# Building the gate matrix of a sparse expert layer with accumulating indirect DMAs instead of one-hot products on TensorE

## The chip, the cores and the metric

The program runs on one core of a Trainium2 chip. A core has TensorE (PE in the rows) for matrix products, VectorE (DVE), ScalarE (ACT), GpSimd (POOL) and SyncE (SP), which share an on-chip memory of 128 partitions (SBUF), PSUM banks for products, and 16 DMA engines. DMAs are issued here by SP (plain loads) and by POOL (gathers by index, and others). The metric is the device time of the whole program in microseconds (us), lower being better.

## The reference, cut to what matters

One decoder layer on 256 tokens of width 2048: a retention group and a sparse-attention group share an input projection, their outputs go through an output projection, and a PEER layer follows. Only the PEER layer is touched. Every token picks, for each of 8 heads, 16 of 128 x 128 experts; expert (i, j) has a row of `u` and a row of `v`.

```python
def peer_ffn(x, wq, subkeys, u, v):
    q = (xt @ wq).reshape(n, PEER_HEADS, 2, PEER_DQ // 2)
    s = jnp.einsum('nhpd,pkd->nhpk', q, subkeys)
    sv, si = lax.top_k(s, PEER_TOPK)
    cand = sv[:, :, 0, :, None] + sv[:, :, 1, None, :]
    cidx = si[:, :, 0, :, None] * PEER_NKEYS + si[:, :, 1, None, :]
    cs, ci = lax.top_k(cand.reshape(n, PEER_HEADS, PEER_TOPK * PEER_TOPK), PEER_TOPK)
    eidx = jnp.take_along_axis(cidx.reshape(...), ci, axis=-1)
    gate = jax.nn.softmax(cs.astype(jnp.float32), axis=-1)
    # per chunk of tokens:
        hid = jax.nn.gelu(jnp.einsum('cd,chkd->chk', xc, u[ec]))
        return jnp.einsum('chk,chkd->cd', gc * hid, v[ec])
```

## The kernel before, in words

**Two ways for the tokens.** 192 tokens (`TD`) are computed densely: all 16384 experts are multiplied with them, and the result is weighted with a gate matrix that is zero where an expert was not picked. The other 64 (`TS`) are computed sparsely: the rows of `u` and `v` that they picked are gathered from DRAM, 128 rows (1 MB) at a time, and VectorE multiplies them.

**The stages of the PEER part.** The 128 values of j are taken in two halves of 64. A half has 64 `u` blocks and then 64 `v` blocks. A `u` block loads 1 MB into one of four `raw` buffers and multiplies it with the tokens (`u_block`, L918, in the first half); ScalarE writes its GELU into `hidden` (L1285). A `v` block loads 1 MB, ScalarE and VectorE split it into a rounded part and a rest (L1318, L1932), and TensorE multiplies both with the gated `hidden` (L1009 to L1021). The gated `hidden` reaches TensorE through `wm`: ScalarE's `round_gated` and VectorE's L1986 and L1987 write it.

**The routing.** During the first 64 `u` blocks VectorE picks the experts. `route_tokens(1, 0)` takes tokens 128 to 255 first, with no gathers between; `route_tokens(0, 14)` takes tokens 0 to 127 and works off 14 gathers (items) at points spread through it (`share`). A token's choice is i (`choice[:, 0]`), j (`choice[:, 1]`) and a gate (`choice[:, 2]`), 128 of each (`SLOTS`).

**The gate matrix.** After `u` block 31 TensorE turns the choices so that a token's 128 choices lie along the partitions (L962), ScalarE copies them out (`choiceT`), and then, for 24 batches of 8 tokens, VectorE writes two one-hot matrices per token (`onehots`, L1902 and L1905), TensorE multiplies them into a 128 x 128 matrix of the token (`gate_batch`, L973, one batch behind each of the `u` blocks 33 to 56), VectorE multiplies columns 0 to 31 straight into `hidden` (`apply_gates`, L1916), and ScalarE copies the other 96 out (`gate_copy`, L1339) so that POOL stores them to DRAM in 12 DMAs (`store_gates`, L568). SP reads them back later in 12 DMAs of 768 KB (`load_gates`), and VectorE multiplies a row of them with a row of `hidden` from `v` block 32 of the first half on (L1967).

**The sparse tokens.** `pair_items` lists 128 items, a gather each: 64 of `u` rows (VectorE L1804) and 64 of `v` rows (L1807). `items_by(b)` says how many are to be issued by block b: 14 in blocks 13 to 31, 24 in blocks 32 to 59, and the others later. POOL issues them in program order in `fetch` (L561); a gather of block b waits until block b - 5 is done (`block_done`) and until its buffer is free, which two buffers in turn make the case two items earlier. VectorE has item 38 behind it, `items_to(items_by(HALF - 1))`, before it starts on the first `v` block.

**What sets the order.** Each engine runs its own list in the order written out by hand in its section of `build`; semaphores tie the lists together. In the first `u` stage POOL's list holds only the gathers and, from block 38 on, the stores between them. `v` block 0 waits on TensorE for `wm_hi` and `wm_lo`, which ScalarE and VectorE raise when its gated row is written.

Of the kernel before, what the change touches and what calls it, by code (L numbers as in the profile page):

```python
# [18 lines left out]
F32 = mybir.dt.float32  # L19
F32R = mybir.dt.float32r  # L20
U32 = mybir.dt.uint32
# [51 lines left out]
GATE_BLOCKS, BATCHES = HALF - ROUTED, TD // 8  # L73
GATED_EARLY = ROUTED
STORED_GROUPS = (NKEYS - GATED_EARLY) // GROUP_J
# [22 lines left out]

def buffer_of(i):
    return i % 2 if i < FIRST_GATHERS else 2 + i % 2 if items_by(HALF + 8) > i else (0, 2, 3)[i % 3]  # L100
# [18 lines left out]

SBUF_0 = 16512  # L120
# [65 lines left out]
def build(nc, a, out):  # L186
    with ExitStack() as ctx:
# [19 lines left out]
        onehots_sb = at("onehots_sb", 20480, [P, 4096])  # L207
# [9 lines left out]
        choiceT = at("choiceT", 50432, [P, 3, T])  # L217
        base = at("base", 51200, [P, 3 * P + 3 * TS])
# [62 lines left out]
        def ysq(c):  # L281
# [21 lines left out]
        onehot = onehots_sb[:, :].rearrange("p (b s n j) -> p b s n j", b=2, s=2, n=8)  # L303
# [10 lines left out]
        gate_dram = nc.dram_tensor("gate_matrix", (STORED_GROUPS, P, TD, GROUP_J), F32, kind="Internal").ap()  # L314
# [30 lines left out]
        res_stored, q_scores, q_copied, route, route_exp, choices_ready, ch_turned, ch_copied = (  # L345
            sem(s) for s in ("res_stored", "q_scores", "q_copied", "route", "route_exp", "choices_ready", "ch_turned", "ch_copied"))
# [7 lines left out]
        gate_applied = sem("gate_applied")  # L354
# [3 lines left out]
        onehots_ready, gate_rows, gate_evac, res_loaded = (  # L358
            sem(s) for s in ("onehots_ready", "gate_rows", "gate_evac", "res_loaded"))
        gate_stored = [sem(f"gate_stored{s}") for s in range(2)]  # L360
# [21 lines left out]
        def _(sp):  # L382
# [70 lines left out]
            for half in range(2):  # L453
# [4 lines left out]
                else:  # L458
# [6 lines left out]
                    sp.wait_ge(gate_rows, BATCHES)  # L465
# [13 lines left out]
                def load_gates(q, g):  # L479
                    sp.dma_start(gs[:, g, 0:TD * GROUP_J], gate_dram[q].rearrange("i t j -> i (t j)")).then_inc(gate_loaded[g], 16)  # L480

                early = GATED_EARLY // GROUP_J if half == 0 else 0
                first = 0 if half == 0 else HALF // GROUP_J - GATED_EARLY // GROUP_J
                for q in range(early):
                    for r in range(GROUP_J):
                        load_v(GROUP_J * q + r, r % RAW)
                    if q == 1:
                        for s in range(2):
                            sp.wait_ge(gate_stored[s], 16 * (TD // 32))
                        for g in range(2):  # L490
                            load_gates(g, g)
                for q in range(early, HALF // GROUP_J):
# [3 lines left out]
                    x = first + q - early  # L496
                    if x >= 2:
                        sp.wait_ge(gated, GROUP_J * (x - 1))
                        load_gates(x, x % 2)
                    for r in range(GROUP_J):  # L500
                        load_v(GROUP_J * q + r, r % RAW)
# [19 lines left out]
        def _(pool):  # L521
# [12 lines left out]

            pool.wait_ge(acc_evacuated, RK + 4)
            half = RET_DK // 2
            for x in range(4):
                pool.dma_start(other_half[half * x:half * (x + 1), :], tile(RQ, 8)[half * (x ^ 1):half * (x ^ 1) + half, :]
                               ).then_inc(halves_swapped, 16)

# [23 lines left out]
            def store_gates(x):  # L564

                pool.wait_ge(gate_evac, 2 * x + 2)
                t0 = 16 * x
                pool.dma_start(gate_dram.rearrange("g i t j -> i g (t j)")[:, :, t0 * GROUP_J:(t0 + 16) * GROUP_J],  # L568
                               gs[:, x % 2, 0:STORED_GROUPS * 16 * GROUP_J].rearrange("p (g n) -> p g n", g=STORED_GROUPS)
                               ).then_inc(gate_stored[x % 2], 16)  # L570
# [20 lines left out]
        def _(pe):  # L591
# [363 lines left out]
            with pe.Fori(1, ROUTED // RAW) as lap:  # L955
                for s in range(RAW):
                    u_block(RAW * lap + s, s)

            pe.wait_ge(choices_ready, 2)
            pe.wait_ge(q_copied, 8)  # L960
            for x in range(6):
                last = nc.tensor.transpose(bank[2 + x // 4][:, (x % 4) * P:(x % 4 + 1) * P], choice[:, x // 2, x % 2, :], ident)  # L962
            last.then_inc(ch_turned, 1)


            def gate_batch(b):

                pe.wait_ge(onehots_ready, b + 1)
                if b >= 2:
                    pe.wait_ge(gate_evac, b - 1)  # L970
                    pe.wait_ge(gate_applied, b - 1)
                for t in range(8):
                    last = mm(bank[4 + 2 * (b % 2) + t // 4][:, (t % 4) * P:(t % 4 + 1) * P],  # L973
                              onehot[:, b % 2, 0, t, :], onehot[:, b % 2, 1, t, :], start=True, stop=True)
                last.then_inc(gate_rows, 1)

            for r in range(GATE_BLOCKS):
                u_block(ROUTED + r, (ROUTED + r) % RAW)
                if 1 <= r <= BATCHES:
                    gate_batch(r - 1)  # L980
                if r == GATE_BLOCKS - 4:
                    pe.wait_ge(gate_evac, BATCHES)
                    pe.wait_ge(gate_applied, BATCHES)
# [4 lines left out]
            for half in range(2):  # L988
# [7 lines left out]
                else:  # L996
                    pe.wait_ge(gate_evac, BATCHES)
                    pe.wait_ge(gate_applied, BATCHES)
# [79 lines left out]
        def _(ac):  # L1078
# [251 lines left out]
            def gate_copy(b):  # L1330

                ac.wait_ge(gate_applied, b + 1)
                if b % 2 == 0 and b >= 4:
                    ac.wait_ge(gate_stored[b // 2 % 2], 16 * (b // 4))
                for x in range(2):
                    dst = gs[:, b // 2 % 2, 0:STORED_GROUPS * 16 * GROUP_J].rearrange("p (g t j) -> p t g j", g=STORED_GROUPS, t=16)
                    t0 = 8 * (b % 2) + 4 * x
                    late = bank[4 + 2 * (b % 2) + x][:, :].rearrange("p (t n) -> p t n", t=4)[:, :, GATED_EARLY:NKEYS]
                    last = do(dst[:, t0:t0 + 4, :, :], late.rearrange("p t (g j) -> p t g j", j=GROUP_J), ACT.Copy)  # L1339
                last.then_inc(gate_evac, 1)  # L1340

            def round_gated(half, mv):

                weights = hidden[:, mv * TD:(mv + 1) * TD]
                if half or mv >= GATED_EARLY:
                    ac.wait_ge(gated, mv + (HALF * half + 1) - GATED_EARLY)
                    weights = wmt[:, (mv % 2) * TD:(mv % 2 + 1) * TD]
# [734 lines left out]
```

## Time and profile before

| | us |
|---|---|
| device time, 3 runs | 1794.59, 1795.06, 1795.17 (median 1795.06) |
| span of the profiled execution | 1793.2 |
| busy: PE, DVE, ACT, POOL | 1774.3 (99%), 1388.5 (77%), 766.7 (43%), 170.8 (10%) |

The profiled execution has no device time of its own in the record; its span lies 1.9 us under the median of the runs. The first `u` stage of the PEER part runs from 516.1 to 901.2 us. In the page, an engine's busy share is the time in which it works on an instruction; instructions that issue DMAs are counted on POOL for the time that they take the engine. The chain of waits follows the work that ended last back to the start.

### The profile page before, as it was taken

How to read it: one execution, taken by the hardware profiler on the slowest of the kernel's cores; microseconds unless marked ns; L12 is line 12 of the kernel's file. 1: busy time of each engine (PE TensorE's matmuls, PEld its weight loads, DVE VectorE, ACT ScalarE, POOL GpSimd, SP SyncE). 2: the span in 40 equal slices, each digit the busy share in tenths (PEclk: the TensorE clock that was granted, in tenths of full speed). 3: DMA queues.
4: the chain of work that ended last, by engine and by line, in shares of the span. 5: the costliest groups of instructions: out<-in, count | busy, mean ns of one | idle time of the engine just before them, and what ended most of it. 6: DMA issues, size and time to landing. Idle time of an engine off the chain costs nothing.

```text
span 1793.2 us, 27943 instructions
## 1 busy us (share of the span) xinstructions
PE 1774.3 (99%) x10680; PEld 1591.7 (89%) x10680; DVE 1388.5 (77%) x2153; ACT 766.7 (43%) x1054; POOL 170.8 (10%) x158
## 2 busy tenths in 40 slices
PE   8999999999999999999999999999999999999998
PEld 8899989789999999999977777789999998777775
DVE  6546667566459796888378898989999998898996
ACT  5334444655331010111155555555555555555555
POOL 0000000000000121222100000111111111111010
PEclk9999999999999999999999999999999999999999
DMA  9774544556545987998999899999999999999984
GB/s 351 262 280 149 165 141 142 188 187 226 187 150 192 358 333 282 342 336 331 362 377 361 317 324 341 344 350 367 377 369 374 377 347 361 353 359 365 357 309 152
DMA packets 77275, 531.01 MB, mean 296 GB/s; under 512 B 8811, under 2 KB 9211, under 8 KB 16268
## 3 DMA queue, kind: packets, MB, share of 16 engines
q1 hardware_dynamic: 54512, 377.96, 56.6%
q0 software_dynamic: 22352, 151.59, 23.2%
q8 instruction: 45, 0.74, 0.2%
q10 hardware_dynamic: 332, 0.44, 0.1%
q14 instruction: 34, 0.28, 0.0%
HBM read 512.60 MB, written 15.20 MB: 294 GB/s over the span
## 4 chain that ended last, share of the span: by engine, by line
PE 97%; DVE 1%; issue 1%; ACT 1%; DMA 0%; DVEq 0%; SPq 0%; ACTq 0%
PE bank L918 19%; PE bank L934 11%; PE bank L596 8%; PE bank L597 8%; PE bank L598 8%; PE bank L1015 6%; PE bank L1014 6%; PE bank L1019 6%; PE bank L1021 6%; PE bank L1020 6%; PE bank L935 5%; PE bank L973 2%; PE bank L743 0%; PE bank L952 0%; PE bank L791 0%
## 5 line engine op out<-in xcount | busy, mean ns | idle before, releaser
L1932 DVE TENSOR_TENSOR lo<-raw,hi 128x1024 fp32r<-128x1024 f32 x384 | 463.6, 1221 | 101.7 <-ACT hi L1318 101.3
L1318 ACT ACTIVATE hi<-raw 128x1024 fp32r<-128x1024 f32 x384 | 404.9, 1059 | 320.8 <-PE bank L1021 233.5
L918 PE MATMUL bank<-hT,raw 128*128 128x192 f32 x2048 | 337.4, 326 | 0.0
L918 PEld LDWEIGHTS bank<-hT,raw 128*128 128x128 f32 x2048 | 332.3, 190 | 0.1
L934 PE MATMUL bank<-xr,hi 128*128 128x384 f32 x1024 | 291.3, 359 | 0.0
L935 PE MATMUL bank<-xr,lo 128*128 128x192 f32 x1024 | 256.3, 250 | 0.0
L1444 DVE TENSOR_TENSOR lo<-raw,hi 128x2048 fp32r<-128x2048 f32 x75 | 171.8, 2290 | 103.7 <-ACT hi L1086 68.2
L1015 PE MATMUL bank<-lo,wm 128*64 128x512 f32 x512 | 202.8, 396 | 0.0
L1014 PE MATMUL bank<-hi,wm 128*128 128x512 f32 x512 | 199.9, 390 | 1.7 <-DVE wm L1987 1.2
L1019 PE MATMUL bank<-lo,wm 128*128 128x512 f32 x512 | 200.3, 391 | 0.0
L1021 PE MATMUL bank<-hi,wm 128*128 128x512 f32 x512 | 199.3, 389 | 0.0
L1020 PE MATMUL bank<-hi,wm 128*128 128x512 f32 x512 | 199.3, 389 | 0.0
L935 PEld LDWEIGHTS bank<-xr,lo 128*128 128x128 f32 x1024 | 195.6, 191 | 0.0
L934 PEld LDWEIGHTS bank<-xr,hi 128*128 128x128 f32 x1024 | 192.2, 188 | 0.0
L1804 DVE SCALAR_TENSOR_TENSOR rows_sb<-rows_sb,xs 128x2048 f32<-128x2048 f32 x64 | 146.3, 2285 | 22.2 <-DMA rows_sb<-in_u_rows,pairs 22.0
L1807 DVE SCALAR_TENSOR_TENSOR acc<-rows_sb,wcol,acc 128x2048 f32<-128x2048 f32 x64 | 150.2, 2347 | 14.1 <-DMA rows_sb<-in_v,pairs 13.5
L1285 ACT ACTIVATE arena<-bank 128x192 f32<-128x192 f32 x64 | 21.1, 330 | 292.3 <-PE bank L918 292.2
L596 PE MATMUL bank<-act,hi 128*128 128x256 f32 x480 | 139.9, 292 | 1.6 <-issue 0.8
L597 PE MATMUL bank<-act,hi 128*128 128x256 f32 x480 | 136.5, 284 | 0.0
L598 PE MATMUL bank<-act,lo 128*128 128x256 f32 x480 | 136.5, 284 | 0.0
L1086 ACT ACTIVATE hi<-raw 128x2048 fp32r<-128x2048 f32 x55 | 105.0, 1909 | 65.1 <-PE bank L598 56.1
L1014 PEld LDWEIGHTS bank<-hi,wm 128*128 128x128 f32 x512 | 96.2, 188 | 38.7 <-issue 4.8
(293 smaller groups left out, 2686.2 us busy)
## 6 DMA issues: line engine op xcount, KB each, us to landing
raw<-in_u SPq DMA_DIRECT2D x128, 1024.0 KB, 7.7
raw<-in_v SPq DMA_DIRECT2D x128, 1024.0 KB, 7.2
raw<-in_w_in SPq DMA_DIRECT2D x43, 1024.0 KB, 5.8
raw<-in_w_out SPq DMA_DIRECT2D x16, 1024.0 KB, 4.8
raw<-in_wq SPq DMA_DIRECT2D x16, 1024.0 KB, 4.8
gate_matrix<-gs POOLq DMA_DIRECT2D x12, 768.0 KB, 12.5
gs<-gate_matrix SPq DMA_DIRECT2D x12, 768.0 KB, 9.2
raw<-in_cmp_w SPq DMA_DIRECT2D x8, 1024.0 KB, 4.8
```

The lines of the kernel that those rows point to most:

```text
L596: mm(dst, wh, mh, start=first, stop=False)
L597: mm(dst, wh, ml, start=False, stop=False)
L918: last = mm(bank[s % 2][:, 0:TD], raw[:, s, k * P:(k + 1) * P], xn[:, k, 0:TD], start=(k == 0), stop=(k == KT - 1))
L934: mm(acc_bank[:, 0:2 * TD], hi[:, s % 2, w], xr[:, k, :], start=(k == 0), stop=False, skip_group_check=True)
L935: last = mm(acc_bank[:, 0:REST_COLS], lo[:, s % 2, w], xr[:, k, 0:REST_COLS], start=False, stop=(k == KT - 1), skip_group_check=True)
L1014: mm(bank[4 + dc][:, :], packed, vh[:, cols], start=False, stop=False, skip_group_check=True)
L1015: return mm(bank[4 + dc][0:TS, :], packed[:, 0:TS], vl[:, cols], start=False, stop=closing, skip_group_check=True)
L1019: mm(bank[dc][:, :], whole, vl[:, cols], start=opening and dc < 2, stop=False, skip_group_check=True)
L1020: mm(bank[dc][:, :], whole, vh[:, cols], start=False, stop=False, skip_group_check=True)
L1021: return mm(bank[dc][:, :], rest, vh[:, cols], start=False, stop=closing, skip_group_check=True)
L1318: do(hi[:, s % 2, cols], raw[:, s, cols], ACT.Copy).then_inc(v_hi_ready, 1)
L1932: vec.tensor_tensor(lo[:, n % 2, cols], raw[:, n % RAW, cols], hi[:, n % 2, cols].bitcast(F32), ALU.subtract).then_inc(v_lo_ready, 1)
```

## The change

The gate matrix is no longer computed. `gate_matrix` in DRAM is now (j, i, token), 128 x 128 x 192 cells. POOL clears it with 8 DMAs during the input projection (`clear`, one behind each fourth block from 12 to 40), from a zeroed tile.

`route_tokens` ends with three more VectorE operations that work out each choice's cell, (j * 128 + i) * 192 + token, into `sidx`, with the gate in `sgate`. Two POOL DMAs copy half of the choices of tokens 128 to 191 from the lower to the upper 64 partitions (`cells_moved`), so that one DMA serves two choices of each of the 64 tokens.

POOL then issues 192 indirect DMAs that add, each, 128 single cells of 4 bytes to the matrix (`add_gate`): 64 for tokens 128 to 191, in blocks 14 to 29, and 128 for tokens 0 to 127, in blocks 32 to 53. A group of tokens has 8 heads, so 8 DMAs for each head of tokens 128 to 191 and 16 for each head of tokens 0 to 127. From the second head on, a head's first DMA waits until all earlier ones of its group have landed: 7 such waits in each group. They stand between the gathers on POOL.

TensorE's 24 batches, the turning, ScalarE's and VectorE's parts of it and the 12 stores go. SP waits for all 192 additions behind its first four `v` loads, then reads the matrix back in 16 DMAs of 768 KB, 8 rows of 768 bytes for each partition. VectorE gates every `v` block's row (128 times instead of 96).

```diff
+ZERO_PARTS, ZERO_W = 8, 2 * TD
+SCATTERS = (SLOTS, SLOTS // 2)
+SCATTER_1, SCATTER_0 = (14, 30), (ROUTED, 54)
...
+            pool.wait_ge(cells_ready, 1)
+            for cells in (sidx, sgate):
+                by_head = cells[:, 1, :].rearrange("p (h k) -> p h k", h=PH)
+                pool.dma_start(by_head[TS:P, :, 0:PK // 2], by_head[0:TS, :, PK // 2:PK]).then_inc(cells_moved, 16)
             pool.wait_ge(pairs_loaded, 32)
...
-            def store_gates(x):
...
+            def add_gate(tt, n):
+
+                per_head = SCATTERS[tt] // PH
+                h, k = n // per_head, n % per_head
+                if n == 0:
+                    pool.wait_ge(cells_ready, 2 - tt)
+                    if tt:
+                        pool.wait_ge(cells_moved, 32)
+                        pool.wait_ge(gate_zeroed, 16 * ZERO_PARTS)
+                elif k == 0:
+                    pool.wait_ge(gates_added[tt], 16 * n)
+                slot = PK * h + k
+                pool.indirect_dma_start(gate_cells, bass.IndirectOffsetOnAxis(ap=sidx[:, tt, slot:slot + 1], axis=0),
+                                        sgate[:, tt, slot:slot + 1], None, compute_op=ALU.add).then_inc(gates_added[tt], 16)
 
             for b in range(PAIRS_LISTED, 4 * HALF):
-                r = b - ROUTED
                 if b == ROUTED:
-                    pool.wait_ge(ch_copied, 3)
+                    pool.wait_ge(cells_ready, 2)
                 if b == HALF + 8:
                     pool.wait_ge(res_added, 6)
-                if 6 <= r < 6 + BATCHES and r % 2 == 0:
-                    store_gates(r // 2 - 3)
+                for tt in (1, 0):
+                    for n in range(scatters_by(tt, b - 1), scatters_by(tt, b)):
+                        add_gate(tt, n)
```

On TensorE, at `u` block 32 (L918 before, L954 now; raw buffers 0, 1, 2 in turn, from block 32 before and from block 60 now). Before:

```order
L962 MATMUL bank<-base,arena 128x128 [waits q_copied,choices_ready]
L962 MATMUL bank<-base,arena 128x128 x5
L918 MATMUL bank<-hT,raw 128x192 [waits acc_evacuated,raw_loaded0]
L918 MATMUL bank<-hT,raw 128x192 x15
L918 MATMUL bank<-hT,raw 128x192 [waits acc_evacuated,raw_loaded1]
L918 MATMUL bank<-hT,raw 128x192 x15
L973 MATMUL bank<-onehots_sb 128x128 [waits onehots_ready]
L973 MATMUL bank<-onehots_sb 128x128 x7
```

Now, the end of the stage, with the only products between blocks (they open six banks, L999), and the first product of `v` block 0:

```order
L954 MATMUL bank<-hT,raw 128x192 [waits acc_evacuated,raw_loaded0]
L954 MATMUL bank<-hT,raw 128x192 x15
L999 MATMUL bank<-hi 128x512 [waits q_copied]
L999 MATMUL bank<-hi 128x512 x5
L954 MATMUL bank<-hT,raw 128x192 [waits acc_evacuated,raw_loaded1]
L954 MATMUL bank<-hT,raw 128x192 x15
L954 MATMUL bank<-hT,raw 128x192 [waits acc_evacuated,raw_loaded2]
L954 MATMUL bank<-hT,raw 128x192 x15
L954 MATMUL bank<-hT,raw 128x192 [waits acc_evacuated,raw_loaded3]
L954 MATMUL bank<-hT,raw 128x192 x15
L1026 MATMUL bank<-hi,wm 128x512 [waits v_hi_ready,wm_lo,v_lo_ready,wm_hi,res_added]
```

The eight products of a batch that stood behind `u` blocks 33 to 56 are gone, and the waits for `onehots_ready` with them.

On POOL, from block 32 on, behind the first 14 gathers (`rows_sb` is a gather's buffer). Before:

```order
L561 DMA rows_sb_63<-in_u_rows,pairs 128x2048 [waits block_done,ch_copied]
L561 DMA rows_sb_64<-in_u_rows,pairs 128x2048 [waits block_done]
L561 DMA rows_sb_63<-in_v,pairs 128x2048 [waits dots_ready,block_done]
L561 DMA rows_sb_64<-in_v,pairs 128x2048 [waits dots_ready,block_done]
L561 DMA rows_sb_63<-in_v,pairs 128x2048 [waits acc_step,block_done]
L568 DMA gate_matrix<-gs 128x12x128 [waits gate_evac]
L561 DMA rows_sb_64<-in_v,pairs 128x2048 [waits acc_step,block_done]
L568 DMA gate_matrix<-gs 128x12x128 [waits gate_evac]
```

Now (L605 is `add_gate`; L590 the gather):

```order
L605 DMA gate_matrix<-sgate,sidx 3145728x1 [waits cells_ready]
L605 DMA gate_matrix<-sgate,sidx 3145728x1 x10
L590 DMA rows_sb_62<-in_u_rows,pairs 128x2048 [waits block_done]
L605 DMA gate_matrix<-sgate,sidx 3145728x1 x5
L605 DMA gate_matrix<-sgate,sidx 3145728x1 [waits gates_added0]
L590 DMA rows_sb_63<-in_u_rows,pairs 128x2048 [waits block_done]
L605 DMA gate_matrix<-sgate,sidx 3145728x1 x6
L590 DMA rows_sb_62<-in_v,pairs 128x2048 [waits dots_ready,block_done]
L605 DMA gate_matrix<-sgate,sidx 3145728x1 x6
L590 DMA rows_sb_63<-in_v,pairs 128x2048 [waits dots_ready,block_done]
```

Between two gathers stand five to twelve additions where a store stood or nothing; behind the last addition six gathers are left before the `v` stage.

On VectorE, at the end of the routing of tokens 0 to 127. Before:

```order
L1885 TENSOR_TENSOR arena<-arena,small 128x128 [waits route]
L1902 TENSOR_TENSOR onehots_sb<-base,choiceT 128x1024 [waits acc_evacuated,ch_copied]
L1905 TENSOR_SCALAR onehots_sb<-base,choiceT 128x128 x8
L1902 TENSOR_TENSOR onehots_sb<-base,choiceT 128x1024
L1905 TENSOR_SCALAR onehots_sb<-base,choiceT 128x128 x8
L1916 TENSOR_TENSOR arena<-bank,arena 128x32x4 [waits gate_rows]
```

Now (L1794 and L1797 are the items):

```order
L1878 SCALAR_TENSOR_TENSOR sidx_f<-arena,sidx_f 128x128 [waits route]
L1881 CAST sidx<-sidx_f 128x128 [waits route]
L1883 TENSOR_TENSOR sgate<-arena,small 128x128 [waits route]
L1794 SCALAR_TENSOR_TENSOR rows_sb_62,hcol<-rows_sb_62,xs 128x2048 [waits rows_fetched2]
L1794 SCALAR_TENSOR_TENSOR rows_sb_63,hcol<-rows_sb_63,xs 128x2048 [waits rows_fetched3]
L1787 TENSOR_TENSOR wcol<-hcol,pairs 128x4 [waits hcol_ready]
L1797 SCALAR_TENSOR_TENSOR acc<-rows_sb_62,wcol,acc 128x2048 [waits acc_step,rows_fetched2,acc_begun,wcol_ready]
```

Behind the routing VectorE now has nothing but the 24 items until the `v` stage.

## Rows read from the trace of the kernel before

**Rows 1.** The page: the chain that ended last, by engine.

```profile
PE 97%; DVE 1%; issue 1%; ACT 1%; DMA 0%; DVEq 0%; SPq 0%; ACTq 0%
```

**Rows 2.** Busy time in four stretches: length, each engine, granted clock, DMA share, GB/s.

```profile
core 0: us, PE busy (x) PEld busy (x) DVE busy (x) ACT busy (x) POOL busy (x), PEclk, DMA share, GB/s
100.00:420.00 320.00, 317.84 (x2046) 283.22 (x2045) 201.74 (x300) 158.30 (x212) 2.00 (x4) 1.00 0.50 177
...
584.00:692.00 108.00, 108.00 (x669) 107.98 (x668) 88.54 (x233) 9.99 (x26) 19.86 (x16) 1.00 0.89 336
692.00:901.00 209.00, 209.00 (x1405) 208.50 (x1404) 147.55 (x307) 35.77 (x94) 43.34 (x37) 1.00 0.90 335
...
900.00:950.00 50.00, 49.98 (x221) 38.63 (x220) 39.01 (x52) 26.48 (x36) 4.93 (x5) 1.00 0.96 361
```

**Rows 3.** The chain in order of time, first `u` stage: start us, us, what.

```profile
689.69 0.66 PE bank L962 x6
...
854.66 1.78 PE bank L973 x16
856.45 5.20 PE bank L918 x32
...
884.24 1.40 PE bank L985 x6
```

**Rows 4.** POOL's groups over the span: busy us, mean ns of one, idle before.

```profile
L561 POOL DMA_INDIRECT rows_sb<-in_v,pairs x64 | 74.4, 1162 | 501.4 <-PE bank L1021 260.8 <-DVE rows_sb L1804 148.1 <-DVE acc L1807 80.2
L561 POOL DMA_INDIRECT rows_sb<-in_u_rows,pairs x64 | 72.6, 1134 | 469.1 <-PE bank L1021 181.8 <-DVE acc L1807 136.5 <-DVE rows_sb L1804 86.7
...
L550 POOL DMA_DIRECT2D pairs<-arena x2 | 1.2, 597 | 72.0 <-DVE arena L1893 72.0
...
L587 POOL DMA_DIRECT2D acc<-acc x1 | 1.0, 956 | 20.3 <-DVE acc L1807 20.3
...
L542 POOL DMA_DIRECT2D g_row<-in_norm_row x1 | 0.5, 521 | 215.5 <-DVE arena L1656 215.5
```

**Rows 5.** POOL in order of time: start us, us, what, idle before.

```profile
587.16 1.04 POOL L561 DMA_INDIRECT rows_sb<-in_u_rows,pairs  x1 [1.52 <-DMA pairs<-arena]
588.50 0.98 POOL L561 DMA_INDIRECT rows_sb<-in_u_rows,pairs  x1 [0.30 <-issue]
597.60 0.94 POOL L561 DMA_INDIRECT rows_sb<-in_u_rows,pairs  x1 [8.13 <-DVE rows_sb L1804]
...
663.21 2.24 POOL L561 DMA_INDIRECT rows_sb<-in_v,pairs  x1 [5.32 <-DVE acc L1807]
...
727.25 1.17 POOL L561 DMA_INDIRECT rows_sb<-in_v,pairs  x1 [6.06 <-DVE acc L1807]
728.43 1.12 POOL L568 DMA_DIRECT2D gate_matrix<-gs  x1
```

**Rows 6.** VectorE in order of time, in the routing of tokens 128 to 255 and 0 to 127.

```profile
583.14 0.29 DVE L1885 TENSOR_TENSOR arena<-arena,small 128x128 f32<-128x128 f32 x1
...
583.61 0.28 DVE L1890 SCALAR_TENSOR_TENSOR arena<-arena 128x128 f32<-128x128 f32 x1
...
662.36 2.28 DVE L1874 TENSOR_TENSOR gs<-gs,arena 128x2048 f32<-128x2048 f32 x1
```

**Rows 7.** VectorE in order of time, the last item and the first `v` block.

```profile
895.38 2.29 DVE L1804 SCALAR_TENSOR_TENSOR rows_sb<-rows_sb,xs 128x2048 f32<-128x2048 f32 x1 [1.71 <-DMA rows_sb<-in_u_rows,pairs]
897.60 0.08 DVE L1804 DVE_READ_ACCUMULATOR rows_sb<-rows_sb,xs 128x1 f32 x1
897.60 2.36 DVE L1932 TENSOR_TENSOR lo<-raw,hi 128x1024 fp32r<-128x1024 f32 x2
```

**Rows 8.** DMA issues of 584 to 692 us: KB each, median us from issue to landing.

```profile
rows_sb<-in_u_rows,pairs POOLq DMA_INDIRECT x10, 9.5
pairs<-arena POOLq DMA_DIRECT2D x2, 32.0 KB, 1.9
```

**Rows 9.** The page: POOL's DMA queue over the span: packets, MB, share of 16 engines.

```profile
q0 software_dynamic: 22352, 151.59, 23.2%
```

**Rows 10.** L1967, the gating of a row: ns min, median and max, first and last start.

```profile
L1967 DVE TENSOR_TENSOR wmt<-arena,gs x96: 499/536/611, 1044.7 to 1770.9; 128x192 f32<-128x192 f32 x96
```

More of the change, by code:

```diff
@@ L96, in items_by, with scatters_by @@
     return sum(n * min(max(b + 1 - first, 0), last - first) // (last - first) for first, last, n in STAGE_ITEMS)
+def scatters_by(tt, b):
+    first, last = (SCATTER_0, SCATTER_1)[tt]
+    return SCATTERS[tt] * min(max(b + 1 - first, 0), last - first) // (last - first)
 def buffer_of(i):
@@ L118, in group_end @@
     return ITEMS.index(("u", GROUP * q + GROUP - 1)) + 1
+FIRST_DOTS = max(j + 1 for i, (kind, j) in enumerate(ITEMS) if i < FIRST_GATHERS and kind == "u")
+FIRST_STEPS = max(j + 1 for i, (kind, j) in enumerate(ITEMS) if i < FIRST_GATHERS and kind == "v")
 SBUF_0 = 16512
@@ L357, in build @@
             sem(s) for s in ("fold_even", "fold_odd", "folded", "fin_added", "fin_shared", "fin_weighted"))
[L358 to L360 removed]
+        res_loaded = sem("res_loaded")
         gate_loaded = [sem(f"gate_loaded{s}") for s in range(2)]
@@ L479, in load_gates @@
                 def load_gates(q, g):
[L480 to L492, printed above, removed]
+                    sp.dma_start(gs[:, g, 0:TD * GROUP_J].rearrange("i (j t) -> i j t", t=TD),
+                                 gate_dram[GROUP_J * q:GROUP_J * (q + 1)].rearrange("j i t -> i j t")).then_inc(gate_loaded[g], 16)
+                if half == 0:
+                    for r in range(RAW):
+                        load_v(r, r)
+                    for tt in range(2):
+                        sp.wait_ge(gates_added[tt], 16 * SCATTERS[tt])
+                    for g in range(2):
+                        load_gates(g, g)
+                for q in range(HALF // GROUP_J):
                     if half and q == 3:
@@ L495, in _ @@
                         sp.dma_start(h_first, res_dram[:, 0:1024]).then_inc(gf_loaded, 16)
-                    x = first + q - early
+                    x = HALF // GROUP_J * half + q
                     if x >= 2:
@@ L539, in _ @@
                                ).then_inc(halves_swapped, 16)
+            for c in range(ZERO_PARTS // 2, ZERO_PARTS):
+                clear(c)
             pool.wait_ge(acc_evacuated, M_WQ)
@@ L954, in _ @@
                         last.then_inc(q_scores, 1)
-            with pe.Fori(1, ROUTED // RAW) as lap:
+            with pe.Fori(1, HALF // RAW - 1) as lap:
                 for s in range(RAW):
                     u_block(RAW * lap + s, s)
[L959 to L983, printed above, removed]
+            for s in range(RAW):
+                u_block(HALF - RAW + s, s)
+                if s == 0:
+                    pe.wait_ge(q_copied, 8)
                     for b in range(2, 8):
@@ L1328, in spread_xn @@
                 do(xr[:, k, 0:TD], src, ACT.Copy).then_inc(xr_hi, 1)
[L1330 to L1340, printed above, removed]
-            def round_gated(half, mv):
[L1344 to L1347, printed above, removed]
-                do(wm[:, mv % 2, 0:TD], weights, ACT.Copy).then_inc(wm_hi, 1)
+            def round_gated(half, mv):
+                ac.wait_ge(gated, mv + (HALF * half + 1))
+                do(wm[:, mv % 2, 0:TD], wmt[:, (mv % 2) * TD:(mv % 2 + 1) * TD], ACT.Copy).then_inc(wm_hi, 1)
             for r in range(1, HALF):
@@ L1385, in _ @@
                         round_split(2 * HALF * half + mv)
-                        if half and mv < 2:
-                            hidden_gelu(HALF - 2 + mv)
-                        round_gated(half, mv)
+                    if half and mv < 2:
+                        hidden_gelu(HALF - 2 + mv)
+                    round_gated(half, mv)
                     pair_gelus((2 * half + 1) * HALF + mv)
```

118 lines of the change are left out of this document (51 added, 67 removed).

## The prediction

> **What bounds the kernel now.** I read the page's chain of waits first: 97% of it is TensorE [rows 1]. Then the stretches: from 584 to 901 us, which is most of the first `u` stage, TensorE is busy throughout at the full granted clock, while POOL is busy 20 of 108 and 43 of 209 us, and the DMA engines 0.89 and 0.90 of the time [rows 2]. The chain in order of time gives the pieces of that stage: a `u` block 5.20 us, a batch of gate products 1.78 us, the turning 0.66 us, the products that open the banks 1.40 us, with no gap between [rows 3]. So a product taken out of this stage shortens it, as long as what `v` block 0 waits for is ready sooner as well. That is the question here: before, VectorE finished its last item at 897.6 us, 3.6 us before the stage's end at 901.2 us [rows 7]. The early end must be reached by POOL, the gathers and VectorE too.
>
> **What the change removes.** 24 batches x 1.78 + 0.66 = 43.4 us of TensorE [rows 3]. It would be done with `u` at 901.2 - 43.4 = 857.8 us; if nothing else were late, the span would be 1793.2 - 43.4 = 1749.8 us. VectorE loses its one-hot matrices and ScalarE its copies; neither is what the end of the stage waits for. The 12 stores go from POOL, 12 x 1.1 us, of which one stands in [rows 5].
>
> **What it adds on POOL.** 192 additions, each an indirect DMA with 128 indices. The nearest row is the gather, also an indirect DMA with 128 indices: 0.94 us when nothing holds it [rows 5], 1.15 us in the mean of all 128 [rows 4]. Between one gather and the next that was ready lie 0.30 us in which POOL waits for nothing (588.50 starts 0.30 after 588.20) [rows 5]; whether this belongs to the indirect DMA or to the gather's waits no row tells, since a store started 0.01 us behind a gather [rows 5]. An accumulating DMA of 64 rows took 0.956 us, a plain one of 64 rows 0.521 [rows 4]: adding may cost 0.43 us more. So an addition costs POOL from 0.94 us to 0.94 + 0.31 + 0.43 = 1.68 us. I take 1.10, halfway between 0.94 and 1.25, without the price of adding, since that rests on a single row.
>
> **What holds POOL besides.** (a) The head waits, 7 + 7. They are bounded by 1.9 us, the landing of a 32 KB copy, and by most of a gather's 9.5 us, since a gather lies in the same queue shortly before [rows 8]. I take 4 us. (b) VectorE. The gather at 663.21 took 2.24 instead of 0.94 us; it began inside VectorE's L1874 (662.36 to 664.64), which reads two operands from SBUF, and ended 0.8 us after it [rows 5, 6]. Before, POOL issued a gather and slept. Now it issues without a pause, so it meets every item, which is an instruction of 2.29 us with two operands [rows 7]. I charge the 1.3 us of this row to each item, and nothing as the lower end. The Trainium skill (SBUF — State Buffer, Who interferes with whom) says that a VectorE instruction with two SBUF inputs and a GpSimd instruction that reads SBUF exclude each other for the whole instruction. The trace agrees in that one row; by the full 2.29 us for each item, 32 items would cost 32 us more and the time would be 1915 us.
>
> **The sum.** It follows POOL through the stage.
> - Start. Before, the first gather went out at 587.2 us. Now VectorE does three more operations first (0.28 each [rows 6]) and POOL two more copies (0.6 each [rows 4]): 589.2.
> - Tokens 128 to 191, with the first 14 gathers between: 64 x 1.10 = 70.4; 14 x 1.25 = 17.5; 7 x 4 = 28; 14 items x 1.3 = 18.2. Sum 134.1, so 723.3.
> - The routing of tokens 0 to 127 has item 14 inside. The last gather lands 9.5 us from its issue at 722.3, the item is 2.29 us and the rest of the routing with the cells' numbers 1.7: cells ready at 735.8. Before, the choices were ready at 689.7 (the turning starts then [rows 3]).
> - Tokens 0 to 127, with 18 gathers between: 128 x 1.10 = 140.8; 18 x 1.25 = 22.5; 28; 18 x 1.3 = 23.4. Sum 214.7, so 950.5.
> - Six gathers are left behind the last addition. They go through two buffers, each round 9.5 + 2.3 = 11.8 us [rows 7, 8]: 3 x 11.8 = 35.4, so 985.9. The read-back of the matrix is done within this time, as stores of the same 768 KB and gathers of 1 MB land in 9 to 13 us.
> - The first `v` block: VectorE's rests 2.36 us [rows 7], the row's gating 0.54 [rows 10] and its part of `wm` 0.5: 3.4, so 989.3.
> TensorE starts on `v` 88.1 us later than before (901.2), and stands idle from 857.8 on. What is queued behind is everything: behind the waiting addition on POOL the gathers, behind these the items and the whole `v` stage on VectorE. Nothing later gives this back, since TensorE is busy 49.98 of 50 us [rows 2]. The span would be 1881.3 us; the runs' median lies 1.9 us over the span, so **1883 us**.
>
> **Edits at next to nothing.** Clearing writes 12.6 MB between blocks 12 and 40, where the DMA engines are busy half the time [rows 2]; I charge 0, and 3 us if a load of a weight block comes late behind it. 32 more gatings of a row on VectorE are 32 x 0.54 = 17 us [rows 10] over 32 blocks in which VectorE is busy 39 of 50 us [rows 2], so hidden. The read-back moves 768-byte pieces instead of 6 KB; it has eight blocks of time for each DMA except the first two.
>
> **The ends of the sum.** Additions at 0.94 us, the rest as above: 192 x 0.16 = 30.7 us less, 1852 us. Without the charge for VectorE as well: 41.6 less, 1811. Additions at 1.25: 28.8 more, 1912. At 1.68: 111 more, 1994.
>
> **Rivals.**
> - *POOL is in time after all, and the kernel is faster.* This needs all lower ends at once: 0.94 us, no blocking by VectorE, and head waits of 1.9 us (14 x 2.1 = 29.4 less than 1811): 1781 us. It decides at about 16 us less than the 1811 case, or an addition that costs about 0.86 us there. For it: most gathers take 0.94 us, and stores followed gathers without a gap. Against: the blocked gathers, and gathers in the same queue ahead of each head wait. Cheaper additions than any row shows would bring it towards 1752 us. Chance 8%.
> - *Adding is dear on POOL.* 1.68 us each gives 1994 us. For it: 0.956 against 0.521 us [rows 4]. Against: one row only, of another form. Chance 15%.
> - *The DMA engines bound it.* An addition is 128 packets of 4 bytes, 8 on each engine. If such a packet, which must read a cell before it writes it, takes what one of 8 KB takes (23.2% x 1793 x 16 / 22352 = 0.298 us [rows 9]), an addition takes 2.4 us, and 192 of them 458 us instead of 211: +247 us, 2130 us at most, less the head waits and blocking that this hides (97 us), so about 2033. It decides from 1.10 / 8 = 0.14 us for a packet. The engines are 0.9 busy already [rows 2]. No row shows such a packet. Chance 13%. The Trainium skill (DMA: Bandwidth & Descriptors, Anatomy of one DMA — SWDGE) gives a fixed cost of about 2.0 us for each DMA; if none of it overlapped, 192 would take 384 us and the time would be an estimated 2056 us; no row here shows how far small DMAs overlap.
> - *The change doesn't take the work off TensorE's path.* Excluded: each batch stands in the chain [rows 3].
>
> **How the numbers follow.** The forecast, 1811 to 1940 us, has 62%; the three rivals 8, 15 and 13%; 2% are left for a time within 0.2% of before, which I take as what a measurement can tell from no change. The range 1811 to 1995 us leaves out the faster cases and the slowest. Faster 0.08, same 0.02, slower 0.90.
>
> **What the profile after would show.** The groups of POOL give an addition's time, and their starts the gap; the idle before a head's first addition gives the head waits; the starts of additions against VectorE's items show the blocking. TensorE should be busy until about 858 us and then idle until about 990, waiting for `wm`, with VectorE waiting for `rows_sb` and POOL busy without a pause. I am wrong if POOL has idle time between heads, if its last addition goes out before 860 us, or if TensorE's idle time lies inside the `u` blocks (loads late because of the small packets).

## The result, and the profile after

The changed kernel takes 2017.3 us (median of four runs, 2014.5 to 2020.2), against 1794.9 us before: a ratio of 1.124, with an interval of 1.122 to 1.126. The direction was forecast, the size was not: 1883 us was predicted, and the range ended at 1995. The profiled execution took 2014.5 us and spans 2012.7. In the changed kernel's numbering an addition is L605, a gather L590, the clearing L553, a `u` block L954, an item on a `u` row L1794 and one on a `v` row L1797, and the copy of a block's result with the gelu, on ScalarE, L1297.

The groups of POOL answer [rows 4]: busy us, mean ns of one, idle before with what ended it.

```profile
L605 POOL DMA_INDIRECT gate_matrix<-sgate,sidx x192 | 318.6, 1659 | 91.4 <-issue 54.3 <-DMA gate_matrix<-sgate,sidx 21.5 <-DVE sgate L1883 10.6
L590 POOL DMA_INDIRECT rows_sb<-in_u_rows,pairs x64 | 77.3, 1207 | 357.6 <-PE bank L1033 177.2 <-DVE acc L1797 106.9 <-DVE rows_sb L1794 31.8
```

POOL in order of time shows what these are made of, and answers [rows 5].

```profile
785.21 1.54 POOL L605 DMA_INDIRECT gate_matrix<-sgate,sidx  x1 [0.30 <-issue]
787.06 1.54 POOL L605 DMA_INDIRECT gate_matrix<-sgate,sidx  x1 [0.30 <-issue]
788.90 1.54 POOL L605 DMA_INDIRECT gate_matrix<-sgate,sidx  x1 [0.30 <-issue]
790.75 0.99 POOL L590 DMA_INDIRECT rows_sb<-in_u_rows,pairs  x1 [0.30 <-issue]
792.05 1.57 POOL L605 DMA_INDIRECT gate_matrix<-sgate,sidx  x1 [0.30 <-issue]
...
797.62 2.55 POOL L605 DMA_INDIRECT gate_matrix<-sgate,sidx  x1 [0.30 <-issue]
...
803.70 1.54 POOL L605 DMA_INDIRECT gate_matrix<-sgate,sidx  x1 [1.69 <-DMA gate_matrix<-sgate,sidx]
```

An addition lasts 1.54 us, and 0.30 us lie between it and the next addition or gather. The starts are 1.85 us apart. A gather in the same run lasts 0.99 us, with the same 0.30. The addition at 797.62 lasted 1.0 us longer than the others; it met this item on VectorE. That at 803.70 is the first of a head and waited 1.69 us.

```profile
796.46 2.29 DVE L1794 SCALAR_TENSOR_TENSOR rows_sb<-rows_sb,xs 128x2048 f32<-128x2048 f32 x1 [26.94 <-DMA rows_sb<-in_u_rows,pairs]
```

The waits between 590 and 1120 us: engine and line, what it waited for, us in total, times, longest.

```profile
ACT hcol L1310 <- DVE rows_sb L1794: 274.8, 5, 84.7
...
PE bank L954 <- ACT arena L1297: 227.0, 5, 75.1
...
DVE rows_sb L1794 <- DMA rows_sb<-in_u_rows,pairs: 206.5, 20, 26.9
```

Read from below it is a chain: gathers come late, so VectorE waits for rows; ScalarE stands in `pair_gelus` (L1310), which needs four dot products of VectorE; behind that waiting instruction stands L1297, which empties the bank of a `u` block; and TensorE waits for the bank. Thus TensorE's idle time lies inside the `u` blocks, 227 us of it, and 15.9 us more ahead of `v` block 0:

```profile
932.28 48.49 PE L954 MATMUL bank<-hT,raw 128*128 128x192 f32 x288 [68.70 <-ACT arena L1297]
1055.88 29.02 PE L954 MATMUL bank<-hT,raw 128*128 128x192 f32 x160 [75.11 <-ACT arena L1297]
...
1119.61 0.76 PE L1026 MATMUL bank<-hi,wm 128*128 128x512 f32 x1 [15.91 <-DVE lo L1906]
```

The stretches answer [rows 2]: length, busy us of each engine, granted clock, DMA share, GB/s.

```profile
60.00:425.00 365.00, 359.79 (x2400) 320.95 (x2399) 218.72 (x313) 169.68 (x218) 10.94 (x14) 1.00 0.61 222
...
592.00:770.00 178.00, 138.78 (x825) 137.90 (x823) 87.75 (x225) 10.77 (x29) 128.84 (x80) 0.89 0.77 242
770.00:1060.00 290.00, 102.20 (x589) 101.61 (x590) 42.03 (x31) 6.55 (x23) 230.30 (x146) 0.66 0.51 130
1060.00:1120.00 60.00, 42.54 (x252) 41.64 (x251) 17.58 (x15) 10.29 (x20) 8.05 (x9) 0.87 0.91 332
```

From 770 to 1060 us POOL is the only engine at work most of the time, and the DMA engines, 0.90 busy in the same stage before, are half idle. `v` block 0 starts at 1119.6 us instead of 901.2: 218.4 us of the 219.5 by which the span grew. From there on the two kernels run alike, 893.1 against 892.0 us.

The last addition ends at 1060.5 us, 59.1 us ahead of `v` block 0. The chain that ended last goes on from there through these pieces: start us, us, what.

```profile
1069.32 18.46 DMA raw<-in_u
...
1087.83 15.88 PE bank L954 x96
...
1104.15 12.25 DMA gs<-gate_matrix
```

### The profile page after: what moved, and what is told of

It reads as the page before. It is cut to its first block, busy times and chain, and to the rows that moved or that the text cites. A ratio compares the mean times of both kernels' runs of the same rounds, so it can differ in the third digit from the quotient of the medians.

```text
span 2012.7 us, 27104 instructions
## 1 busy us (share of the span) xinstructions
PE 1746.0 (87%) x10290; PEld 1561.4 (78%) x10290; DVE 1294.9 (64%) x1931; ACT 745.8 (37%) x1003; POOL 486.3 (24%) x348
## 3 DMA queue, kind: packets, MB, share of 16 engines
q0 software_dynamic: 50512, 154.88, 24.3%
## 4 chain that ended last, share of the span: by engine, by line
PE 74%; POOL 13%; issue 5%; DMA 5%; DVE 2%; ACT 1%; SPq 0%; DVEq 0%; POOLq 0%; ACTq 0%
POOL gate_matrix L605 12%; PE bank L970 10%; PE bank L954 7%; PE bank L632 7%; PE bank L633 7%; PE bank L634 7%; PE bank L1027 6%; PE bank L1026 6%; PE bank L1031 6%; PE bank L1032 6%; PE bank L1033 6%; PE bank L971 5%; DMA rows_sb<-in_u_rows,pairs 1%; POOL rows_sb L590 1%; DMA gate_matrix<-sgate,sidx 1%
## 5 line engine op out<-in xcount | busy, mean ns | idle before, releaser
L954 PE MATMUL bank<-hT,raw 128*128 128x192 f32 x2048 | 345.7, 333 | 228.6 <-ACT arena L1297 227.0
L954 PEld LDWEIGHTS bank<-hT,raw 128*128 128x128 f32 x2048 | 343.5, 195 | 230.5 <-ACT arena L1297 228.5
L605 POOL DMA_INDIRECT gate_matrix<-sgate,sidx x192 | 318.6, 1659 | 91.4 <-issue 54.3
L1794 DVE SCALAR_TENSOR_TENSOR rows_sb<-rows_sb,xs 128x2048 f32<-128x2048 f32 x64 | 146.4, 2288 | 206.5 <-DMA rows_sb<-in_u_rows,pairs 206.5
L1797 DVE SCALAR_TENSOR_TENSOR acc<-rows_sb,wcol,acc 128x2048 f32<-128x2048 f32 x64 | 150.3, 2349 | 160.8 <-DMA rows_sb<-in_v,pairs 160.4
L1026 PE MATMUL bank<-hi,wm 128*128 128x512 f32 x512 | 200.3, 391 | 17.3 <-DVE lo L1906 15.9
L590 POOL DMA_INDIRECT rows_sb<-in_v,pairs x64 | 71.2, 1113 | 426.5 <-PE bank L1033 261.3
L590 POOL DMA_INDIRECT rows_sb<-in_u_rows,pairs x64 | 77.3, 1207 | 357.6 <-PE bank L1033 177.2
L1026 PEld LDWEIGHTS bank<-hi,wm 128*128 128x128 f32 x512 | 96.4, 188 | 54.2 <-issue 20.3
```

What stands on the lines that cost most here:

```text
L605: pool.indirect_dma_start(gate_cells, bass.IndirectOffsetOnAxis(ap=sidx[:, tt, slot:slot + 1], axis=0), sgate[:, tt, slot:slot + 1], None, ...
L954: last = mm(bank[s % 2][:, 0:TD], raw[:, s, k * P:(k + 1) * P], xn[:, k, 0:TD], start=(k == 0), stop=(k == KT - 1))
L1026: mm(bank[4 + dc][:, :], packed, vh[:, cols], start=False, stop=False, skip_group_check=True)
```

## The experiments

### Without additions, and with half of them

The first takes the calls of `add_gate` and SyncE's wait for them out:

```
-                for tt in (1, 0):
+                for tt in ():
                     for n in range(scatters_by(tt, b - 1), scatters_by(tt, b)):
                         add_gate(tt, n)
```

> Left out: the 192 additions; the gate matrix stays zero, so the experts add nothing. Everything else stays (clearing, cell numbers, read-back, order of blocks). Theory A (POOL's time per addition, 1.54 us and 0.30 us behind it, is the loss): POOL is free again, the first u stage goes at TensorE's pace, v block 0 starts at 901.2 + 5.1 (the clearing) - 43.4 (products gone) = 863, and the kernel takes 863 + 893 + 1 = 1757 us. Theory B (something else of the change holds TensorE too: the layout of the read-back, the later gate loads, VectorE's new steps): TensorE still waits ahead of the v stage and the time stays above 1800 us.

Measured: 1770.7 us, 0.986 of before (0.984 to 0.987). Theory A holds for the bulk: the additions cost the changed kernel 246.6 us. TensorE has no idle time in the `u` blocks, and `v` block 0 starts at 876.7 us. That is 14 us later than expected, and the chain says why: start us, us, what.

```profile
847.64 15.61 PE bank L954 x96
863.27 0.33 SPq L458
863.64 9.88 DMA gs<-gate_matrix
873.54 0.36 DVE wmt L1939
873.90 2.28 DVE lo L1906 x2
```

SyncE issues the first gates behind the first `v` loads, of which the last waits for a `u` block's end. The read-back begins when the stage is over, and TensorE stands 13.5 us. The kernel before needed no stored gates for its first 32 `v` blocks.

The second leaves out every other addition (`if k % 2: return` in `add_gate`, with the counts that are waited for halved).

> Left out: every second addition of each head, 96 of 192, so half of the gates are missing; the waits between heads stay. Theory A (every addition costs POOL 1.85 us and nothing takes its place): stage 0 has 64 additions fewer, 118 us, and POOL is no longer behind when the second cells come, so the time falls by 118 us plus what stage 1 was behind, 40 to 60 us: 1840 us (1810 to 1870). Theory C (the waits between heads, or the blocks after which additions are placed, set POOL's pace): 16 waits stay, and the time falls by less than 80 us, to 1940 us or more.

Measured: 1864.1 us, ratio 1.039 (1.037 to 1.041): within theory A's range, against C. The first 96 additions cost 93 us over the kernel without any, the other 96 cost 153 us, 1.60 us each. An addition costs less than its 1.85 us while POOL has some idle time left.

### What an addition's time is made of

Once without `compute_op=ALU.add`, once with 64 of the 128 partitions (`sidx[0:64, ...]`, `sgate[0:64, ...]`).

> The 192 transfers write their gates to the cells instead of adding them, so where two heads hit one cell the later gate stands alone. Theory A1 (the sum in the transfer is what makes POOL's part long, against a gather's 0.99 us): a transfer's record falls from 1.54 to 0.95 to 1.05 us, 192 x 0.55 = 105 us less, and the kernel takes 1900 us (1885 to 1920). Theory A2 (the price is that of an indirect write of 4-byte cells, adding or not): the record stays at 1.5 us and the time at 2017 us. In both the 0.30 us of issue behind each stay.

> Each of the 192 additions takes 64 partitions instead of 128, so the upper half of the gates is left out. If POOL's part is made of a price for each index: a record falls from 1.54 to 0.8 to 1.0 us, 192 x 0.6 = 115 us less, 1900 us. If it is a fixed price of the instruction: the record stays within 0.1 us of 1.54 and the time within 1% of 2017 us. The 0.30 us of issue behind each stay in both.

Measured, two runs each: 1925.4 us (ratio 1.072, 1.069 to 1.076) and 1996.5 us (1.112, 1.109 to 1.115). POOL in order of time, the plain write first, then the half:

```profile
914.49 0.96 POOL L605 DMA_INDIRECT gate_matrix<-sgate,sidx  x1 [0.30 <-issue]
915.75 0.96 POOL L605 DMA_INDIRECT gate_matrix<-sgate,sidx  x1 [0.30 <-issue]
```

```profile
909.87 1.41 POOL L605 DMA_INDIRECT gate_matrix<-sgate,sidx  x1 [0.30 <-issue]
911.58 1.41 POOL L605 DMA_INDIRECT gate_matrix<-sgate,sidx  x1 [0.30 <-issue]
```

A plain write costs what a gather costs. Adding puts 0.58 us on it, 111 us for 192, of which 92 reach the kernel's time. The record of theory A1 holds; its time doesn't, 1925 us against 1885 to 1920. Half the indices save 0.13 us of 1.54, a little more than the 0.1 us allowed for a fixed price, and the time is 1.0% lower. So all 128 indices would be 0.26 us (an estimate, if each costs the same), and five sixths of the record are the instruction's own: what counts is mostly the number of transfers. A plain write also makes 32 packets (POOL's queue: 29008 in all, 22864 without additions) where an addition makes 144 and its half form 80 (38224). By the half form's 0.002 us for each packet, 112 more of them would be 0.23 of the 0.58 us, an estimate; the rest goes with adding. The 0.30 us stay in all forms. The changed kernel's additions already use all 128 partitions (192 tokens x 128 gates = 192 x 128).

### The clearing alone

The eight clearing transfers, the memset that they read and POOL's wait for them, added to the kernel before.

> The kernel before with nothing of the change but the eight clearing transfers (12.6 MB of zeros into a matrix that nobody reads), issued after the same blocks. Theory D (the 5.1 us by which the u stage starts later in the changed kernel are the clearing's): 1800 us, +4 to +6 us. Theory D0 (they come from something else of the change, and the clearing is free as the prediction charged it): within 1 us of the kernel before.

Measured: 1800.5 us against 1794.9, ratio 1.0030 (1.0018 to 1.0042). The stretches of this kernel:

```profile
60.00:425.00 365.00, 359.92 (x2396) 321.22 (x2395) 217.76 (x313) 168.69 (x216) 10.96 (x14) 0.99 0.62 222
425.00:520.00 95.00, 94.93 (x778) 94.08 (x777) 54.57 (x59) 37.41 (x34) 3.48 (x4) 1.00 0.60 208
```

TensorE is busy 359.9 of the first 365 us (359.8 in the changed kernel); in the kernel before it is 362.8, with a DMA share of 0.54. Theory D holds: the clearing costs 5.6 us.

The trace also shows where. The products that start at 125.4 us in the kernel before (L758) start at 131.4 us here and 130.5 us in the changed kernel, and those that start at 306.2 us (L820) at 312.3 and 311.3 us. So the whole loss arises before 131 us, behind the first of the eight transfers, issued at 90.4 us. Between 90 and 110 us the kernel before already has a DMA share of 0.80. A weight load that now lands late holds TensorE for 2.9 us, after which its granted clock falls to 0.63 for 110 to 115 us:

```profile
91.98 11.26 DMA raw<-in_w_in
```

```profile
100.00:105.00 5.00, 4.75 (x48) 3.96 (x46) 0.00 (x0) 1.66 (x1) 0.00 (x0) 1.00 1.02 425
105.00:110.00 5.00, 2.32 (x11) 2.35 (x12) 2.63 (x2) 1.60 (x2) 0.00 (x0) 0.69 1.00 406
110.00:115.00 5.00, 5.00 (x30) 5.00 (x30) 2.29 (x1) 0.56 (x1) 0.00 (x0) 0.63 0.37 151
```

The seven transfers from 123 to 298 us, where the DMA share without them is 0.47, cost nothing. Whether a later place for the first would save the 5.6 us was not tried.

### Where the additions stand

The first experiment keeps the 64 additions of the first stage and leaves out the 128 of the second; the second spreads these 64 over three times as many blocks.

```
-SCATTER_1, SCATTER_0 = (14, 30), (ROUTED, 54)
+SCATTER_1, SCATTER_0 = (14, 62), (ROUTED, 54)
```

> Left out: the 128 additions of the second stage (tokens 0 to 127 get no gates); the 64 of the first stage stay where they are. Theory A: POOL's 64 x 1.85 = 118 us lie between 598 and about 740 and delay that stage's gathers, and with them ScalarE and TensorE; TensorE stalls there (28 us of the 100 in 600:700 in the changed kernel) and the stall can't be made up: 28 to 35 us above the kernel without additions, 1800 to 1806 us. Rival: the gathers catch up when the additions are through and TensorE loses nothing: 1771 to 1778 us, and then 64 additions could be had beside the other work.

> Left out as in the kernel with the first cells only: the 128 additions of the second stage. Its 64 additions, placed there after blocks 14 to 29 (four to eight between two gathers), stand after blocks 14 to 61, one to three between two gathers. Without additions POOL idles 4 to 7 us ahead of nearly every gather, waiting for VectorE to free a row buffer. Theory G (an addition costs nothing while it fits into that idle time, 1.85 us each against 4.3 us and more, and its full price as soon as it doesn't): the 72 us that these 64 additions cost go almost wholly, 1771 to 1785 us. Theory H (each addition delays the gather behind it, which has no slack, wherever it stands): the 72 us stay, 1830 to 1845 us.

Measured: 1842.6 us (ratio 1.026, 1.024 to 1.027), then 1780.8 us (0.991, 0.989 to 0.993). So 64 additions cost 72 us in a burst and 10 us spread. The stretches from 592 to 770 us, burst and then spread:

```profile
592.00:770.00 178.00, 138.16 (x820) 136.98 (x818) 80.32 (x210) 10.68 (x29) 132.67 (x79) 0.90 0.75 234
```

```profile
592.00:770.00 178.00, 176.42 (x1086) 176.13 (x1085) 106.72 (x231) 13.94 (x39) 109.17 (x65) 1.00 0.94 337
```

Up to 770 us all 64 additions have been issued in the first run and 41 in the second; POOL is busy 133 and 109 us, and TensorE loses 40 us and 2 us. My expectation of the burst was 28 to 35 us: it took one part of the stall, the 28 us from 600 to 700 us in the changed kernel. The delayed gathers don't catch up: each waits for VectorE to free one of two buffers, mostly 4 to 7 us behind the last gather, so in the burst run 22 us more of TensorE's idle time follow between 770 and 900 us, after the last addition. The pace of the items has little slack. Theory G holds for this run: an addition is almost free as long as it fits between two gathers. Of the 10 us that are left, TensorE's waits show 1.6 and 4.2 us inside the `u` blocks, and 19.0 us ahead of `v` block 0 where the run without additions has 13.5.

The other question was whether TensorE's stalls inside the `u` blocks are a loss of their own. The 128 additions of the second stage were put after blocks 46 to 61 (`SCATTER_0 = (46, 62)`).

> Nothing left out; the 128 additions of the second stage are placed after blocks 46 to 61 instead of 32 to 53. Theory A (POOL's sum sets the end, wherever the additions stand): additions still begin near 770 us, POOL's sum is the same, and only the six gathers behind the last addition, and the blocks that wait for them, move ahead of it: 1970 to 1990 us. Theory F (TensorE's stalls inside the u stage, through ScalarE's hcol step, are a loss of their own, which gathers ahead of the additions would save): 1900 us or less.

Measured: 2010.5 us, ratio 1.122 (1.120 to 1.124). TensorE's waits in 590 to 1120 us:

```profile
PE bank L954 <- ACT arena L1297: 125.5, 4, 77.0
...
PE bank L1026 <- DVE lo L1906: 114.2, 1, 114.2
```

Together 239.7 us, against 227.0 + 15.9 = 242.9 us. Some 100 us of the idle time have moved from the `u` blocks to the place where I had forecast it, and the total stands. Theory F falls. Theory A holds in that the additions' place hardly matters, but its 1970 to 1990 us don't: the second additions began at 823 us and not near 770, since POOL first stands in the gathers' waits for VectorE. So the gathers that were moved ahead saved 7 us in all.

### The gates' loads ahead of the `v` loads

SyncE's two `load_gates` with their wait were put ahead of the first four `load_v`, without additions and then with all of them.

> As the kernel without additions (they are left out here too), and SyncE issues the first two loads of gates ahead of the first v loads instead of behind them. Theory E (the 13.5 us in which TensorE stands ahead of v block 0 there are the read-back, queued behind the v loads): they go, 1757 us. Rival (that wait is the v data's own: transfers are short of DMA engines, .98 busy in 700:860): the gates come sooner and the v loads later, and the time stays within 4 us of 1771.

> The changed kernel with the first two loads of gates ahead of the first v loads on SyncE, nothing else: the wait for the additions then stands ahead of the v loads. Theory E (as in the kernel without additions, the read-back stands queued behind v loads that wait for the last blocks; here the last addition ends 43 us before the gates are loaded): the 12 us of the read-back and its last wait go, 2003 to 2007 us. Rival (v data is then what comes last, since its loads are now behind the additions): within 4 us of 2017.

Measured: 1759.2 us (ratio 0.980, 0.979 to 0.982) and 2014.8 us (1.122, 1.120 to 1.124). Without additions theory E holds: 11.6 of the 13.5 us go. With all of them the rival holds. The chain there ends with the loads that have now moved behind:

```profile
1081.28 18.21 DMA raw<-in_u
1100.36 17.35 DMA raw<-in_v
```

The last `u` loads wait for the late blocks, the gates' loads stand behind them, and the `v` loads behind these. The read-back, which ended the changed kernel's chain, is followed here by the `v` loads, and they end no sooner.

### A third of the tokens by additions

Spread additions being nearly free, I built the kernel before with tokens 128 to 191 by additions and tokens 0 to 127 by one-hot products.

```
-GATE_BLOCKS, BATCHES = HALF - ROUTED, TD // 8
+GATE_BLOCKS, BATCHES = HALF - ROUTED, P // 8
+ADD_AT = (14, 54)
+CLEARS, ZERO_W = 4, 256
...
+            for g in range(4):
+                rows = gs[:, 0, 512 * g:512 * (g + 1)].rearrange("p (t j) -> p j t", j=GROUP_J)
+                last = vec.tensor_tensor(part[:, g, :, P:TD], rows, part[:, g, :, P:TD], ALU.mult)
```

> Nothing left out. The gates of tokens 128 to 191 go by additions (64 of them, one to two between two gathers, placed after the gather of blocks 14 to 53), those of tokens 0 to 127 by one-hot products as in the kernel before: 16 batches instead of 24, a third of the cells to clear, and VectorE multiplies the first 32 keys' cells of these 64 tokens into the hidden rows at the end of the u stage. Theory G (64 additions fit into POOL's idle time if spread): 8 x 1.78 = 14.2 us of TensorE go, 5.6 / 3 = 1.9 us of clearing come, and 0 to 6 us of additions that don't fit: 1783 to 1789 us, faster than the kernel before by 0.3 to 0.7%. Theory H (even spread, the additions delay gathers that TensorE waits for in the end, as the 10 us left over in the run with spread additions): 1793 us or more.

Measured: 1811.4 us, ratio 1.010 (1.008 to 1.012), slower than before. Theory H holds here. The 14.2 us of products are gone, yet TensorE is idle where it never was:

```profile
600.00:700.00 100.00, 91.35 (x563) 91.05 (x561) 78.31 (x187) 9.02 (x23) 68.86 (x38) 0.97 0.94 326
...
860.00:900.00 40.00, 31.51 (x169) 30.94 (x170) 19.31 (x14) 2.31 (x8) 4.73 (x5) 0.87 0.93 333
```

Its longest waits in the stage are 8.9 us for the choices of tokens 0 to 127, whose routing on VectorE waits for late items, 5.7 us for a `u` load, and 4.6 us for ScalarE, which waits for late items: the mechanism of theory H. The batches put their own work on VectorE and need the choices in time; the run with spread additions had neither. That this is why its 10 us could not be carried over is argued, not shown. Other places for these 64 additions were not tried, and no version here beats the kernel before with the whole work done.

## Why the prediction was wrong

By its own steps:

- **What bounds the kernel, and what the change removes**: right. Without the rest, 1795 - 43.4 + 5.6 (clearing) is 1757 us, and the run without additions, gates first, took 1759.
- **The start**: 598.1 us for the first addition, where 589.2 stood. 5.1 us of this is the clearing, charged at 0 (or 3 if a weight load came late, which is what happened), and 3.8 us are left for the copies of the cells, whose landing I left out; POOL waited 5.05 us for it.
- **An addition's price is the step that failed.** I took 1.10 us; it is 1.54 + 0.30, with starts 1.85 us apart, and 192 x 0.75 is 144 us. [rows 4] and [rows 5] held all three pieces: 0.94 for a gather, 0.30 ahead of a gather that was ready, and 0.43 by which an accumulating DMA was dearer than a plain one. I treated the second as probable by half and put the third aside, because it rested on one row. The upper end of 1.68 added all three and was close (the price of adding is 0.58, not 0.43), and the rival built on it, at 15%, named the true mechanism. The 0.30 us go with the indirect DMA and stand ahead of it. In the changed kernel they are there ahead of additions that wait for no semaphore. In the kernel before, a plain store starts 0.00 or 0.01 us behind a gather, but a gather that was ready starts 0.30 us behind a store:

```profile
869.43 1.08 POOL L568 DMA_DIRECT2D gate_matrix<-gs  x1
870.81 0.97 POOL L561 DMA_INDIRECT rows_sb<-in_u_rows,pairs  x1 [0.30 <-issue]
```

So the store behind a gather, which I took as evidence against the gap, said nothing on two indirect DMAs in a row.

- **Head waits**: I took 14 x 4 = 56 us; 12 waits took 21.5 us in all, with the 0.30 us that stand ahead of any addition. Over-estimated by 35 us, which hid part of the error above.
- **VectorE's blocking**: 32 x 1.3 = 41.6 us were charged. The additions took 318.6 us, 22.9 over 192 x 1.54, and the 32 gathers between them 8.2 us over 0.99 each: 31 us, some 10 less than charged. The 32 items that I counted did run in this time; 25 additions of 1.9 to 3.2 us and 7 gathers of 1.35 to 2.6 us lie beside an item or one of the routing's instructions of 2.3 us. The trace agrees in kind with the Trainium skill's rule (SBUF — State Buffer, Who interferes with whom): the addition at 797.62 ended only 1.4 us behind the item that it met.
- **The path**: the sum followed POOL, which was right: first stage 148.8 us (with 12 of the 14 gathers counted in it) against 134.1, second 290.2 against 214.7. TensorE was to be busy until 858 us and idle after. Instead it stalls in the `u` blocks, as ScalarE stands in `pair_gelus` ahead of emptying a bank. I had named this as a sign of being wrong, but for another reason (late loads). For the time it hardly matters, as the late additions showed. It matters for the **tail**: behind the last addition I counted 38.8 us, six gathers and the first row's work; it took 59.1, since `u` blocks, their loads (18.5 us in the chain) and, last in SyncE's queue, the gates (12.3 us) were also left.
- **Rivals.** The DMA engines as the bound (13%) fall: their share is 0.51 from 770 to 1060 us. "In time after all" (8%) falls. The Trainium skill's 2.0 us for each DMA (DMA: Bandwidth & Descriptors, Anatomy of one DMA — SWDGE) gave an estimated 2056 us, nearer than my sum. That is luck: what queues here is POOL's own 1.85 us, not the transfers, and half the cells in each transfer took only 21 us off.

Of the 130 us between forecast and measured start of `v` (88.1 and 218.4), 8.9 are the start, 14.7 the first stage, 10.9 the way from there to the second cells (23.4 us where 12.5 stood), 75.5 the second stage and 20.3 the tail.

## What to carry to other kernels

Price a new instruction with every part that the nearest rows show, the gap ahead of it included, and add the parts up; leave one out only for a reason, not because a single row carries it. An engine that looks idle (POOL, 43 of 209 us) may be the feeder of a chain with little slack. The same 64 additions, 118 us of POOL, cost 72 us in a burst and 10 us spread; but where other engines needed the chain's results at fixed points, in the last experiment, spreading them was not enough. When the feeder is late, look at what stands in order behind each waiting instruction, down to the last load in the queue, to size the tail.

## What the runs showed of the hardware

- An indirect DMA with 128 indices of 4 bytes keeps POOL for 0.96 us as a write and 1.54 us as an addition; 64 indices instead of 128 save 0.13 us of the addition. Ahead of each that is ready lie 0.30 us in which POOL starts nothing, behind an indirect DMA as behind a store; a store starts 0.00 to 0.01 us behind a gather.
- The transfers are cheap where POOL is dear. Against the kernel without additions, POOL's queue has 192 x 144 = 27648 packets more (50512, not 22864), and its share of the 16 engines went from 23.6% of 1770.7 us to 24.3% of 2012.7 us: about 1140 engine-us, some 0.04 us for each packet, against the 0.298 us that I used for [rows 9].
- 12.6 MB of zeros in eight transfers cost 5.6 us, all of it behind the first, where the DMA share was 0.80 without it. The seven at a share of 0.47 cost nothing.
- TensorE restarts at a lower clock. After 15.9 us without work the first `v` products took 0.63 us each for 3 us (granted clock 0.50), then 0.39 (0.99); the granted clock was 0.66 from 770 to 1060 us, the mean of stretches at 2.4 GHz and at 1.2 GHz. Five `u` blocks took 29.0 instead of 26.0 us behind a pause of 75 us, and the same behind one of 10.4 us.
